# A decoder layer on eight cores: the weight tiles become one stream, and each load is queued when its slot is released

## The chip, the cores and the metric

The kernel runs on the 8 cores of one Trainium2 chip. Every core runs the same program on its own tokens, and no core waits for another. The metric is the device time of the slowest core in microseconds (us); the median of three runs before the change is 3491.16 us (3490.33 to 3492.99).

## The reference

One layer of a hybrid decoder, and a final norm:

```
x += 0.5 * SwiGLU(rms(x)) @ w_down                     # FFN1, width 5632
h  = rms(x);  p = h @ w_in                             # u, v, glu_a, glu_b, gate_a, gate_b
u  = gelu(ua);  v = layer_norm(gelu(va))
y_a = (u * (causal W_s per head and 128-chunk @ v + b_s)) @ w_pa
g  = glu_a * sigmoid(glu_b)                            # 2048 channels
c  = silu(layer_norm(depthwise_conv(g, 31 taps)))      # causal; sample rows take their past from cache_conv
y_b = c @ w_pb
x += (sig(gate_a) * y_a + sig(gate_b) * y_b) @ w_out
x += 0.5 * SwiGLU(rms(x)) @ w_down                     # FFN2
y  = rms(x)
```

The model width is 2048. There are 4 prompts of 2048 tokens and 128 running sequences of 4 new tokens. The outputs are y, the last rows of v and the last 30 rows of the convolution's input.

## The kernel before

Each core holds 1118 tokens (1024 of a prompt, 64 of samples, 30 that the convolution needs from the half prompt before) as columns of [channel, token] tiles, in three segments s = 0, 1, 2 of 364, 364 and 390 columns. All tiles lie in one SBUF tensor, `arena`, and all PSUM banks in `ps`, so these are the names that the profile prints. `mm`, `act`, `tt` and `stt` are helpers that record one operation each; so nearly every matmul has line 192, and every DMA of the program has line 949.

**Weights.** They stream from DRAM (f32) into four SBUF slots (bf16, 128x4096) with DMAs issued by GpSimd (POOL). `wload` (lines 217 to 220) takes the next slot of the ring and queues, on POOL, the wait for the matmul that released that slot and then the DMA. It is called where the tile's use is written; POOL's queue runs in the order in which it was written.

**Stages.** FFN1 (gate-up and down tiles), then the GLU with the convolution, then v (`w_v`), u (`w_u`) with the spatial product, then the gates and both branch projections (`w_gate`, `w_pab`), `w_out`, FFN2. POOL issues weight loads in all of them, and besides them only the small tables `mskc` and `wp` in FFN1 and the convolution's cache rows, below.

**GLU and convolution** (lines 456 to 585), for 16 channel tiles c. GLU(c) is 96 matmuls with the weight tile `w_glu[c]`: for each segment the gate half, then the linear half, multiplied on VectorE into `GP[c % 3]`. `glu_out(c)` writes that tile to DRAM (`gd`) and the state rows to `cst`; `glu_in()` reads it back in four DMAs, shuffled over the partitions, into `GPB[c % 3]`. conv(c) is 72 matmuls over `GPB` and `GS`; its result goes to DRAM (`cd`) and comes back in four DMAs. All of these are issued by SyncE (SP), whose queue is also in written order with its waits: write of `gd`, wait, 4 reads, then write of `cd` once conv is evicted, wait, 4 reads. `conv_weights(c)` (VectorE, two operations of 128x2304) builds the convolution's stationary operand. `conv_cache(c)` is a POOL DMA of the cache rows, `arena<-cachep`, into `GS[c % 3]`; it waits until the convolution that used this buffer, three tiles earlier, is done (`gs_free`).

The order of the stage is written out by hand: GLU(0) to GLU(2) run segment by segment on three tiles held at once, then `conv_cache` for 0, 1 and 2; then for c = 3 to 15 this loop, in which c = 4 and c = 5 run two convolutions each and every other c runs one:

```
for c in range(SKEW, KC):                    # 570
    wi, slot, lev = wload(w_glu[c], 4096)
    ...                                      # GLU(c)
    for cc in order.get(c, [c - 1]):
        conv(cc)
        ...
            cg[cc + 3] = conv_cache(cc + 3)  # 584
```

Of the kernel before, what the change touches and what calls it, by code (L numbers as in the profile page):

```python
# [11 lines left out]
KC = 16  # L12
# [13 lines left out]
SKEW = 3  # L26
# [72 lines left out]
def build_program():  # L99
# [42 lines left out]
    P = Plan()  # L142

    with nc.sbuf_tensor("arena", [128, ARENA_B // 4], F32) as arena, \
# [69 lines left out]
        def pvc(g, k):  # L214
            return PV[:, g * 16 + k:g * 16 + k + 1]

        def wload(src, n, after=()):
            idx, slot, free = wring.get()
            ev = P.dma("pool", slot[:, 0:n], src, "w%d" % idx, deps=free + list(after))
            return idx, slot, ev  # L220

        def wk(slot):
            return slot[:, 0:4096].rearrange("p (k n) -> p k n", n=256)
# [58 lines left out]
                steps.pop(0)()  # L282


        def ffn(w_gu, w_dn, segs, Hv, HID, Xs, hready, seg_steps, tail_steps, dn_seg, x_final, hook, first_order):
            hid = {}
            hid_free = {0: None, 1: None, 2: None}

            def unit(slot, lev, jj, s, steps):
                x0, n = segs[s]  # L290
                W = wk(slot)
                gi_, bg, gfree = banks.get()
                ui_, bu, ufree = banks.get()
                lg = lu = None
                for k in range(KC):
                    lg = mm(bg[:, 0:n], W[:, k, 0:128], Hv[:, k, x0:x0 + n], k == 0, k == KC - 1,
                            deps=[lev, hready[(s, k)]] + (gfree if k == 0 else []))
# [12 lines left out]
                return lu  # L310

            def down(W, m, mi, s, lev):
                x0, n = segs[s]
                bi, bk, bfree = banks.get()
                ld = None
                for jj in range(11):
                    ld = mm(bk[:, 0:n], W[:, jj, mi * 128:(mi + 1) * 128], HID[:, jj, x0:x0 + n], jj == 0, jj == 10,
                            deps=[lev, hid[s]] + (bfree if jj == 0 else []))
                ed = stt(Xs[s][:, m, 0:n], bk[:, 0:n], 0.5, Xs[s][:, m, 0:n], ALU.mult, ALU.add, deps=[ld])
                banks.release(bi, [ed])  # L320
                hid_free[s] = ld
                return ld, ed

            for gi in range(4):
                if gi == 0:
                    held = []
                    for jj in range(SKEW):
                        held.append(wload(w_gu[jj], 4096, after=hook("w", jj)))
                        hook("wl", jj, held[jj][2])
                    for (s, jj) in first_order:  # L330
                        wi, slot, lev = held[jj]
                        if (s, jj) == (1, 0):
                            run_steps(seg_steps.get(1, []), 99)
                        if (s, jj) == (2, 0):
                            run_steps(seg_steps.get(2, []), 99)
                        nxt = 1 if (s, jj) in first_order[:first_order.index((1, 0))] else 2
                        lu = unit(slot, lev, jj, s, seg_steps.get(nxt, []) if s < 2 else [])
                        if s == 2:
                            wring.release(wi, [lu])
                for jj in range(SKEW if gi == 0 else 0, 11):  # L340
                    wi, slot, lev = wload(w_gu[gi * 11 + jj], 4096)
                    lu = None
                    for s in range(3):
                        lu = unit(slot, lev, jj, s, [])
                    wring.release(wi, [lu])
                nm = 8 if gi < 3 else 8 - dn_seg
                for mp in range(nm):
                    wi, slot, lev = wload(w_dn[gi * 8 + mp], 2816)
                    W = slot[:, 0:2816].rearrange("p (j n) -> p j n", n=256)
                    ld = None  # L350
                    for mi in range(2):
                        for s in range(3):
                            ld, ed = down(W, mp * 2 + mi, mi, s, lev)
                            if gi == 3:
                                x_final[(s, mp * 2 + mi)] = ed
                    wring.release(wi, [ld])
                hook("g", gi)
                if gi == 3:
                    held = []
                    for mp in range(nm, 8):  # L360
                        held.append((mp,) + wload(w_dn[gi * 8 + mp], 2816))
                    for s in range(3):
                        for (mp, wi, slot, lev) in held:
                            W = slot[:, 0:2816].rearrange("p (j n) -> p j n", n=256)
                            for mi in range(2):
                                ld, ed = down(W, mp * 2 + mi, mi, s, lev)
                                x_final[(s, mp * 2 + mi)] = ed
                                if s > 0:
                                    run_steps(tail_steps[s - 1], 3)
                            if s == 2:  # L370
                                wring.release(wi, [ld])
                        if s > 0:
                            run_steps(tail_steps[s - 1], 99)
                        hook("s", s)
# [11 lines left out]
        def hook1(what, i, ev=None):  # L386
# [37 lines left out]
            return []  # L424

        run_steps(steps1[0], 99)
        ffn(w_gu1, w_dn1, SEG_A, H, HID1, X1, h1, {1: steps1[1], 2: steps1[2]}, stepsm, DN_SEG, x1f, hook1,
            [(0, 0), (0, 1), (1, 0), (1, 1), (0, 2), (1, 2), (2, 0), (2, 1), (2, 2)])


# [118 lines left out]
                          cd[c].rearrange("(i c) g n -> g c i n", i=4)[g], "cr%d" % (c % 4), deps=[wv])  # L549
            cn_ev[c] = r  # L550

        held = [wload(w_glu[c], 4096) for c in range(SKEW)]
        for s in range(3):
            for c in range(SKEW):
                wi, slot, lev = held[c]
                la = glu_unit(c, slot, lev, s, stepsm[2])
                if s == 2:
                    wring.release(wi, [la])
                    if c == 0:
                        x1_dead = [hm[(0, 15)], hm[(1, 15)], hm[(2, 15)]] + list(sp_ev.values())  # L560
                    glu_out(c)
                    glu_in()
# [5 lines left out]
        cw[1] = conv_weights(1)  # L568
        order = {3: [0], 4: [1, 2], 5: [3, 4]}
        for c in range(SKEW, KC):  # L570
            wi, slot, lev = wload(w_glu[c], 4096)
            la = None
            for s in range(3):
                la = glu_unit(c, slot, lev, s, [])
            wring.release(wi, [la])
            glu_out(c)
            glu_in()
            for cc in order.get(c, [c - 1]):
# [117 lines left out]
                                deps=[e, e_mv])  # L696

        for nb in range(8):
            wi, slot, lev = wload(w_v[nb], 4096)
            W = wk(slot)  # L700
            lm = None
            for (t, rows, hc) in vt:
# [10 lines left out]
                if nb >= 1:  # L713
                    if side:
                        run_steps(side, 3)
                    else:
                        run_steps(side_b, 1)
            wring.release(wi, [lm])
        run_steps(side, 99)
        run_steps(side_b, 99)  # L720

# [75 lines left out]
            u_free[c % 2] = [us_ev[c]]  # L797

        for cp_ in range(8):
            wi, slot, lev = wload(w_u[cp_], 4096)  # L800
            W = wk(slot)
            lm = None
            for ci in range(2):
# [7 lines left out]
                if c == 2:  # L811
                    od8 = v_out(VT[1], 64, vsamp_o, e_vt8, "o_vs")
                    us_after = [od7, od8]
            wring.release(wi, [lm])
        spatial(KC - 1)


# [4 lines left out]
        m_ev = None  # L822
        lya = None
        for c in range(KC):
            w2i, slot2, lev2 = wload(w_gate[c], 4096)
            w1i, slot1, lev1 = wload(w_pab[c], 4096)
            W1 = wk(slot1)
            W2 = wk(slot2)
            for s in range(3):
# [27 lines left out]
                banks.release(yai, [e1])  # L857
                SAR.release(sai, [e1])
                m_ev = tt(MM_[:, c, x0:x0 + n], ta[:, 0:n], tb[:, 0:n], ALU.add, deps=[e1, e2])
            wring.release(w2i, [lgb])  # L860
            wring.release(w1i, [lya])


        rl = {}
# [19 lines left out]

        OUT_SEG = 3
        for mp in range(8 - OUT_SEG):
            wi, slot, lev = wload(w_out[mp], 4096)
# [4 lines left out]
            wring.release(wi, [lm])  # L892
        held = [(mp,) + wload(w_out[mp], 4096) for mp in range(8 - OUT_SEG, 8)]
        for s in range(3):
            for (mp, wi, slot, lev) in held:
                for mi in range(2):
# [1 line left out]
                    if s > 0:  # L898
                        run_steps(steps2[s - 1], 3)
                if s == 2:  # L900
                    wring.release(wi, [lm])
            if s > 0:
                run_steps(steps2[s - 1], 99)

# [5 lines left out]
        def hook2(what, i, ev=None):  # L910
            return []

        ffn(w_gu2, w_dn2, SEG_B, H2, HID2, X2, h2, {1: steps2[2]}, stepsf, 3, x3f, hook2,
            [(s, jj) for s in range(3) for jj in range(SKEW)])
        run_steps(stepsf[2], 99)
        for s in range(3):
# [180 lines left out]
```

How the kernel before makes its waits and increments, by code:

```python
            def emit(eng, e):  # L935
                for item in P.q[eng]:
                    if item[0] == "wait":
                        k, v = item[1], item[2]
                        if k in esem:
                            e.wait_ge(esem[k], sigval[k][v])
                        else:
                            e.wait_ge(dsem[k], v)
                    elif item[0] == "op":
                        ins = item[1](e)
                        idx = item[2]
                        if eng in sigval and idx in sigval[eng]:
                            ins.then_inc(esem[eng], 1)
                    else:
                        ins = e.dma_start(out=item[1], in_=item[2])
                        ins.then_inc(dsem[item[3]], 16)
```

## Time and profile before

| | |
|---|---|
| median of the runs (range) | 3491.16 us (3490.33 to 3492.99) |
| the profiled execution: its own time, span of its slowest core | 3496.27 us, 3494.7 us |
| spans of the eight cores | 3480.9 to 3494.7 us |
| TensorE (PE) busy | 3253.0 us, 93% |
| VectorE (DVE), ScalarE (ACT), GpSimd (POOL) busy | 856.9, 466.4, 128.1 us |
| mean granted TensorE clock | 0.966 |

The span is from the first to the last instruction on core 2, the slowest in this execution. PE is busy nearly all the time, so the time of the kernel is that of PE's work plus the idle time in front of it. "A <- B" in a row is: A was idle and B was what it waited for last. A granted clock of 1.00 is 2.4 GHz, one of 0.50 is 1.2 GHz.

### The profile page before, as it was taken

The numbers are of one execution on the slowest core, as the hardware profiler recorded it, in microseconds if no ns is written. First come the engines' busy times: TensorE is split into PE (matmuls) and PEld (weight loads), VectorE is DVE, ScalarE is ACT, GpSimd is POOL, SyncE is SP. The second block draws the span as 40 slices with busy tenths as digits, with TensorE's granted clock in tenths as the row PEclk, the third lists the DMA queues.
The fourth block names the chain that finished last, engine by engine and source line by source line (L and its number), as shares of the span: only waits on it lengthen the run. The fifth ranks groups of instructions, "written<-read, shape, count | busy, mean of one in ns | idle before, by whom it ended". The sixth has DMA issues, their size and how long they took to land.

```text
span 3494.7 us, 51300 instructions; the slowest of 8 cores (3480.9 to 3494.7 us)
## 1 busy us (share of the span) xinstructions
PE 3253.0 (93%) x21555; PEld 2067.1 (59%) x21556; DVE 856.9 (25%) x1448; ACT 466.4 (13%) x909; POOL 128.1 (4%) x246
## 2 busy tenths in 40 slices
PE   6999999999999756579899999999999999999997
PEld 2566666666665434347756666666666666666664
DVE  2212122121126221222643111112412112112115
ACT  3000000000003100014721000000300000000002
POOL 0000000000000000000000000000000000000000
PEclk9999999999999878789999999999999999999998
DMA  6436434334345343352344334337333434434434
GB/s 155 74 61 123 80 59 81 69 66 85 66 103 127 67 85 55 78 115 59 65 87 73 71 70 71 71 69 177 58 72 71 84 63 78 73 58 82 73 63 119
DMA packets 74112, 284.30 MB, mean 81 GB/s; under 512 B 9888, under 2 KB 36768, under 8 KB 52000
## 3 DMA queue, kind: packets, MB, share of 16 engines
q0 software_dynamic: 34848, 216.62, 35.6%
q1 hardware_dynamic: 39040, 64.40, 6.3%
q8 instruction: 176, 2.88, 0.3%
q14 instruction: 48, 0.39, 0.0%
HBM read 468.14 MB, written 32.87 MB: 143 GB/s over the span
## 4 chain that ended last, share of the span: by engine, by line
PE 91%; DMA 5%; DVE 2%; ACT 1%; issue 1%; POOL 0%; SPq 0%; DVEq 0%; ACTq 0%; POOLq 0%
PE ps L192 91%; DMA arena<-w_glu 4%; ACT arena L195 1%; DVE arena L205 1%; DMA arena<-xin 1%; ACT L195 0%; DVE arena L209 0%; DVE arena L198 0%; DMA vsamp<-arena 0%; DMA arena<-gd 0%; POOL arena L949 0%; DMA gd<-arena 0%; SPq L949 0%; DVEq L940 0%; DVE arena L201 0%
## 5 line engine op out<-in xcount | busy, mean ns | idle before, releaser
L192 PE MATMUL ps<-arena 128*128 128x364 bf16 (+5 forms) x21555 | 3253.0, 313 | 220.7 <-DMA arena<-w_glu 141.6
L192 PEld LDWEIGHTS ps<-arena 128*128 128x128 bf16 (+1 forms) x21556 | 2067.1, 98 | 1406.5 <-issue 282.4
L198 DVE TENSOR_TENSOR arena<-arena,ps 128x364 bf16<-128x364 f32 (+9 forms) x472 | 237.0, 515 | 1838.9 <-PE ps L192 1836.4
L195 ACT ACTIVATE arena<-ps 128x364 f32<-128x364 f32 (+1 forms) x528 | 241.5, 463 | 2574.4 <-PE ps L192 2524.5
L205 DVE SCALAR_TENSOR_TENSOR arena<-ps,arena 128x364 f32<-128x364 f32 (+5 forms) x451 | 241.1, 539 | 501.2 <-PE ps L192 500.9
L198 DVE TENSOR_TENSOR arena<-arena 128x512 bf16<-128x512 f32 (+7 forms) x168 | 185.3, 1115 | 67.3 <-PE ps L192 44.2
L195 ACT ACTIVATE arena<-arena 128x364 bf16<-128x364 f32 (+6 forms) x276 | 152.8, 631 | 268.5 <-PE ps L192 191.7
L205 DVE SCALAR_TENSOR_TENSOR arena<-arena 128x364 bf16<-128x364 f32 (+4 forms) x196 | 101.2, 594 | 1.8 <-DVE arena L209 0.2
L949 POOL DMA_DIRECT2D arena<-w_gu x88 | 46.6, 529 | 1173.3 <-PE ps L192 1132.8
L949 POOL DMA_DIRECT2D arena<-w_dn x64 | 33.8, 528 | 773.8 <-PE ps L192 761.6
L195 ACT ACTIVATE arena<-ps,arena 128x272 bf16<-128x272 f32 (+3 forms) x76 | 38.0, 500 | 102.9 <-PE ps L192 102.8
L209 DVE RECIPROCAL arena<-arena 128x364 f32<-128x364 f32 (+4 forms) x14 | 36.6, 2612 | 42.6 <-ACT arena L195 42.6
L198 DVE TENSOR_TENSOR arena<-ps,arena 128x364 f32<-128x364 f32 (+1 forms) x48 | 24.9, 534 | 87.2 <-PE ps L192 70.0
L195 ACT ACT_TABLE_LOAD x29 | 37.2, 1283 | 62.1 <-PE ps L192 48.2
L691 DVE BATCH_NORM_STATS2 arena<-arena 128x6 f32<-128x256 bf16 (+1 forms) x72 | 26.9, 411 | 59.8 <-ACT arena L195 59.8
L949 POOL DMA_DIRECT2D arena<-cachep x16 | 8.5, 530 | 426.6 <-PE ps L192 386.6
L949 POOL DMA_DIRECT2D arena<-w_gate x16 | 8.4, 528 | 369.2 <-PE ps L192 369.2
L949 POOL DMA_DIRECT2D arena<-w_pab x16 | 8.4, 528 | 91.3 <-PE ps L192 91.3
L949 POOL DMA_DIRECT2D arena<-w_glu x16 | 8.6, 536 | 41.8 <-PE ps L192 41.6
L949 POOL DMA_DIRECT2D arena<-w_u x8 | 4.2, 528 | 153.3 <-PE ps L192 153.3
L949 POOL DMA_DIRECT2D arena<-w_v x8 | 4.3, 538 | 147.2 <-PE ps L192 147.2
L201 DVE TENSOR_SCALAR arena<-ps 128x364 f32<-128x364 f32 (+1 forms) x3 | 1.6, 536 | 31.2 <-PE ps L192 31.2
(10 smaller groups left out, 15.9 us busy)
## 6 DMA issues: line engine op xcount, KB each, us to landing
arena<-w_gu POOLq DMA_DIRECT2D x88, 1024.0 KB, 8.1
arena<-w_dn POOLq DMA_DIRECT2D x64, 704.0 KB, 6.2
arena<-w_glu POOLq DMA_DIRECT2D x16, 1024.0 KB, 11.7
arena<-w_gate POOLq DMA_DIRECT2D x16, 1024.0 KB, 8.7
arena<-w_pab POOLq DMA_DIRECT2D x16, 1024.0 KB, 9.8
arena<-w_v POOLq DMA_DIRECT2D x8, 1024.0 KB, 9.6
arena<-w_u POOLq DMA_DIRECT2D x8, 1024.0 KB, 8.1
arena<-w_out POOLq DMA_DIRECT2D x8, 1024.0 KB, 10.3
```

The lines of the kernel that those rows point to most:

```text
L192: return P.op("pe", lambda e: e.matmul(out, lhsT, rhs, start=start, stop=stop), deps)
L195: return P.op("act", lambda e: e.activation(out=out, in_=in_, func=func, **kw), deps)
L198: return P.op("dve", lambda e: e.tensor_tensor(out=out, in0=in0, in1=in1, op=op), deps)
L201: return P.op("dve", lambda e: e.tensor_scalar(out=out, in0=in0, scalar1=s1, scalar2=s2, op0=op0, op1=op1), deps)
L205: return P.op("dve", lambda e: e.scalar_tensor_tensor(out=out, in0=in0, scalar=scalar, in1=in1, op0=op0, op1=op1), deps)
L209: return P.op("dve", lambda e: e.reciprocal(out=out, in_=in_), deps)
L691: e = P.op("dve", lambda e, t=t, rows=rows, nb=nb: e.bn_stats(out=VST[0:rows, t, nb * 6:nb * 6 + 6], in_=V[0:rows, t, nb * 256:(nb + 1) * ...
L949: ins = e.dma_start(out=item[1], in_=item[2])
```

## The change

The order of all 252 weight tiles is written down once (`wseq`). `wissue` queues the next tile's load; `wnext` hands out the oldest tile that was issued; `wdone` releases a slot and calls `wissue` right there. The first four loads are queued at the start of FFN1, and from then on each load is queued where the slot that it takes is released: four tiles ahead of its use. No operation is added or removed on any engine, and the number and size of the slots stay. What moves is where the loads stand in POOL's queue, relative to `mskc`, `wp` and `cachep`.

```diff
-        def wload(src, n, after=()):
-            idx, slot, free = wring.get()
-            ev = P.dma("pool", slot[:, 0:n], src, "w%d" % idx, deps=free + list(after))
-            return idx, slot, ev
+        wseq = []
+        for gu, dn in ((w_gu1, w_dn1), (None, None), (w_gu2, w_dn2)):
+            if gu is None:
+                wseq += [(w_glu[c], 4096) for c in range(KC)]
...
+        wahead = []
+
+        def wissue(after=()):
+            if wseq:
+                src, n = wseq.pop(0)
+                idx, slot, free = wring.get()
+                wahead.append((idx, slot, P.dma("pool", slot[:, 0:n], src, "w%d" % idx, deps=free + list(after))))
+
+        def wnext():
+            return wahead.pop(0)
+
+        def wdone(idx, events):
+            wring.release(idx, events)
+            wissue()
...
-                        held.append(wload(w_gu[jj], 4096, after=hook("w", jj)))
+                        if not wahead:
+                            wissue(hook("w", jj))
+                        held.append(wnext())
                         hook("wl", jj, held[jj][2])
+                    if not wahead:
+                        wissue()
...
-        held = [wload(w_glu[c], 4096) for c in range(SKEW)]
+        held = [wnext() for c in range(SKEW)]
         for s in range(3):
             for c in range(SKEW):
                 wi, slot, lev = held[c]
                 la = glu_unit(c, slot, lev, s, stepsm[2])
                 if s == 2:
-                    wring.release(wi, [la])
+                    wdone(wi, [la])
...
         for c in range(SKEW, KC):
-            wi, slot, lev = wload(w_glu[c], 4096)
+            wi, slot, lev = wnext()
             la = None
             for s in range(3):
                 la = glu_unit(c, slot, lev, s, [])
-            wring.release(wi, [la])
+            wdone(wi, [la])
```

The other uses of `wload` and `wring.release` become `wnext` and `wdone` in the same way.

POOL's queue of before, from the end of FFN1's loads to the loop's c = 8; `s_pe` is a wait for TensorE, `s_dve` for VectorE, `d_xs..` for the DMAs that save x1 to DRAM:

```order
L949 DMA arena<-w_glu 128x4096 [waits s_pe] x3
L949 DMA arena<-cachep 128x512 [waits s_dve,d_xsa0,d_xsa1,d_xsa2,d_xsb0,d_xsb1,d_xsb2]
L949 DMA arena<-cachep 128x512 x2
L949 DMA arena<-w_glu 128x4096 [waits s_pe]
L949 DMA arena<-cachep 128x512 [waits s_pe]
L949 DMA arena<-w_glu 128x4096
L949 DMA arena<-cachep 128x512 [waits s_pe] x2
L949 DMA arena<-w_glu 128x4096
L949 DMA arena<-cachep 128x512 [waits s_pe] x2
L949 DMA arena<-w_glu 128x4096
L949 DMA arena<-cachep 128x512 [waits s_pe]
L949 DMA arena<-w_glu 128x4096
```

The same place in POOL's queue of the changed kernel:

```order
L976 DMA arena<-w_glu 128x4096 [waits s_pe] x7
L976 DMA arena<-cachep 128x512 [waits s_dve,d_xsa0,d_xsa1,d_xsa2,d_xsb0,d_xsb1,d_xsb2]
L976 DMA arena<-cachep 128x512 x2
L976 DMA arena<-w_glu 128x4096 [waits s_pe]
L976 DMA arena<-cachep 128x512 [waits s_pe]
L976 DMA arena<-w_glu 128x4096 [waits s_pe]
L976 DMA arena<-cachep 128x512 [waits s_pe] x2
L976 DMA arena<-w_glu 128x4096 [waits s_pe]
L976 DMA arena<-cachep 128x512 [waits s_pe] x2
L976 DMA arena<-w_glu 128x4096 [waits s_pe]
```

Seven `w_glu` loads instead of three now stand ahead of the first cache rows. A load that follows a cache row has a wait for TensorE of its own (its slot's release, GLU(c)); before, it had none left, because the cache row just ahead of it had already waited for something later, the end of a convolution. The loads `w_glu[4]` to `w_glu[14]` each stood behind the cache row whose convolution ended just before the load was needed; now the load that follows that row is for a tile four further on.

The end of the loop, in POOL's queue of before:

```order
L949 DMA arena<-w_glu 128x4096
L949 DMA arena<-cachep 128x512 [waits s_pe]
L949 DMA arena<-w_glu 128x4096
L949 DMA arena<-cachep 128x512 [waits s_pe]
L949 DMA arena<-w_glu 128x4096 x2
L949 DMA arena<-w_v 128x4096 x2
L949 DMA arena<-w_v 128x4096 [waits s_pe] x6
```

And of the changed kernel:

```order
L976 DMA arena<-w_glu 128x4096 [waits s_pe]
L976 DMA arena<-cachep 128x512 [waits s_pe]
L976 DMA arena<-w_v 128x4096 [waits s_pe]
L976 DMA arena<-cachep 128x512 [waits s_pe]
L976 DMA arena<-w_v 128x4096 [waits s_pe]
L976 DMA arena<-cachep 128x512 [waits s_pe]
L976 DMA arena<-w_v 128x4096 [waits s_pe] x6
```

`w_v[0]` and `w_v[1]` move ahead of the last two cache rows; `w_v[2]` and all later loads stand behind the same work as before. The queues of TensorE, VectorE, ScalarE and SyncE have the same instructions in the same order in both kernels.

## Rows read from the trace of the kernel before

**Rows 1.** All cores: span and mean granted clock.

```profile
core 2: 3494.7 us, clock 0.966
core 3: 3490.3 us, clock 0.966
```

**Rows 2.** Waits of PE, whole span: total us, times, longest us.

```profile
PE ps L192 <- DMA arena<-w_glu: 141.6, 11, 13.5
PE ps L192 <- ACT arena L195: 46.2, 19, 7.8
...
PE ps L192 <- DMA arena<-gd: 8.6, 1, 8.6
```

**Rows 3.** Chain of waits, 1290 to 1350 us: start us, us, what.

```profile
1299.00 11.86 DMA arena<-w_glu
...
1311.10 21.66 PE ps L192 x168
```

**Rows 4.** Timeline of POOL, 1294 to 1312 us: start us, us, operation, idle before.

```profile
1298.48 0.53 POOL L949 DMA_DIRECT2D arena<-cachep  x1 [33.83 <-PE ps L192]
1299.00 0.54 POOL L949 DMA_DIRECT2D arena<-w_glu  x1
```

**Rows 5.** Windows after one stall: busy us per engine, then clock, DMA share, GB/s.

```profile
1311.00:1314.00 3.00, 2.90 (x10) 1.48 (x11) 0.00 (x0) 0.00 (x0) 0.00 (x0) 0.50 0.00 1
...
1318.00:1323.00 5.00, 5.00 (x34) 3.12 (x33) 0.93 (x2) 0.47 (x1) 0.00 (x0) 1.00 0.02 3
```

**Rows 6.** Windows: from GLU(3)'s end to GLU(14)'s, and on to GLU(15)'s.

```profile
1142.50:1540.40 397.90, 256.28 (x1994) 168.87 (x1993) 95.62 (x103) 41.16 (x85) 14.78 (x28) 0.80 0.41 77
1540.40:1560.40 20.00, 20.00 (x170) 13.65 (x169) 7.79 (x9) 3.39 (x7) 0.00 (x0) 1.00 0.53 113
```

**Rows 7.** Timeline of SP's queue on core 2, 1538 to 1563 us.

```profile
1540.42 0.34 SPq L949 DMA_DIRECT2D gd<-arena  x1
...
1550.46 1.74 SPq L949 DMA_DIRECT2D arena<-gd  x4
1552.30 0.38 SPq L949 DMA_DIRECT2D cd<-arena  x1
1554.61 1.73 SPq L949 DMA_DIRECT2D arena<-cd  x4
1560.43 0.34 SPq L949 DMA_DIRECT2D gd<-arena  x1
```

**Rows 8.** The same queue on core 2, 1130 to 1150 us: GLU(3)'s write.

```profile
1142.50 0.34 SPq L949 DMA_DIRECT2D gd<-arena  x1
```

**Rows 9.** The same queue on core 3: the writes of GLU(3) and of GLU(14).

```profile
1144.13 0.34 SPq L949 DMA_DIRECT2D gd<-arena  x1
...
1536.11 0.34 SPq L949 DMA_DIRECT2D gd<-arena  x1
```

**Rows 10.** Timeline of PE, 1505 to 1605 us: conv(12) alone.

```profile
1504.80 4.89 PE L192 MATMUL ps<-arena 128*128 128x256 bf16 x71
```

**Rows 11.** Timeline of POOL, 1538 to 1582 us: the load issued at GLU(14)'s end.

```profile
1539.62 0.53 POOL L949 DMA_DIRECT2D arena<-w_v  x1 [26.75 <-PE ps L192]
```

**Rows 12.** Tile w_v, 1512 to 1513 us: third and fourth of four loads in a row.

```profile
DMA to landing us min/median/max: 24.6/26.9/29.2
```

**Rows 13.** DMAs, 1540 to 1560 us: median us from issue to landing last.

```profile
arena<-w_v POOLq DMA_DIRECT2D x1, 1024.0 KB, 10.4
gd<-arena SPq DMA_DIRECT2D x1, 280.0 KB, 9.9
arena<-gd SPq DMA_DIRECT2D x4, 70.0 KB, 2.0
```

**Rows 14.** Tile cd, 1302 to 1306 us: four reads beside a weight load.

```profile
DMA to landing us min/median/max: 7.0/7.3/7.4
```

**Rows 15.** Chain of waits, 1500 to 1580 us: the last step of GLU(15)'s round trip.

```profile
1565.66 6.68 DMA arena<-gd
```

**Rows 16.** Windows: FFN1, PE without a gap.

```profile
97.00:1058.00 961.00, 960.89 (x6078) 587.49 (x6078) 173.66 (x315) 67.84 (x142) 39.58 (x75) 1.00 0.44 82
```

More of the change, by code:

```diff
@@ L215, in pvc @@
             return PV[:, g * 16 + k:g * 16 + k + 1]
-        def wload(src, n, after=()):
-            idx, slot, free = wring.get()
-            ev = P.dma("pool", slot[:, 0:n], src, "w%d" % idx, deps=free + list(after))
-            return idx, slot, ev
+        wseq = []
+        for gu, dn in ((w_gu1, w_dn1), (None, None), (w_gu2, w_dn2)):
+            if gu is None:
+                wseq += [(w_glu[c], 4096) for c in range(KC)]
+                wseq += [(w_v[c], 4096) for c in range(8)] + [(w_u[c], 4096) for c in range(8)]
+                for c in range(KC):
+                    wseq += [(w_gate[c], 4096), (w_pab[c], 4096)]
+                wseq += [(w_out[c], 4096) for c in range(8)]
+            else:
+                for gi in range(4):
+                    wseq += [(gu[gi * 11 + jj], 4096) for jj in range(11)]
+                    wseq += [(dn[gi * 8 + mp], 2816) for mp in range(8)]
+        wahead = []
[9 more added lines that the diff above has]
+            wissue()
         def wk(slot):
@@ L282, in run_steps, with ffn @@
                 steps.pop(0)()
-        def ffn(w_gu, w_dn, segs, Hv, HID, Xs, hready, seg_steps, tail_steps, dn_seg, x_final, hook, first_order):
+        def ffn(segs, Hv, HID, Xs, hready, seg_steps, tail_steps, dn_seg, x_final, hook, first_order):
             hid = {}
@@ L338, in ffn @@
                         if s == 2:
-                            wring.release(wi, [lu])
+                            wdone(wi, [lu])
                 for jj in range(SKEW if gi == 0 else 0, 11):
-                    wi, slot, lev = wload(w_gu[gi * 11 + jj], 4096)
+                    wi, slot, lev = wnext()
                     lu = None
@@ L344, in ffn @@
                         lu = unit(slot, lev, jj, s, [])
-                    wring.release(wi, [lu])
+                    wdone(wi, [lu])
                 nm = 8 if gi < 3 else 8 - dn_seg
                 for mp in range(nm):
-                    wi, slot, lev = wload(w_dn[gi * 8 + mp], 2816)
+                    wi, slot, lev = wnext()
                     W = slot[:, 0:2816].rearrange("p (j n) -> p j n", n=256)
@@ L355, in ffn @@
                                 x_final[(s, mp * 2 + mi)] = ed
-                    wring.release(wi, [ld])
+                    wdone(wi, [ld])
                 hook("g", gi)
@@ L360, in ffn @@
                     for mp in range(nm, 8):
-                        held.append((mp,) + wload(w_dn[gi * 8 + mp], 2816))
+                        held.append((mp,) + wnext())
                     for s in range(3):
@@ L370, in ffn @@
                             if s == 2:
-                                wring.release(wi, [ld])
+                                wdone(wi, [ld])
                         if s > 0:
@@ L426, in build_program @@
         run_steps(steps1[0], 99)
[L427 removed]
+        ffn(SEG_A, H, HID1, X1, h1, {1: steps1[1], 2: steps1[2]}, stepsm, DN_SEG, x1f, hook1,
             [(0, 0), (0, 1), (1, 0), (1, 1), (0, 2), (1, 2), (2, 0), (2, 1), (2, 2)])
@@ L570, in build_program @@
         for c in range(SKEW, KC):
-            wi, slot, lev = wload(w_glu[c], 4096)
+            wi, slot, lev = wnext()
             la = None
@@ L698, in build_program @@
         for nb in range(8):
-            wi, slot, lev = wload(w_v[nb], 4096)
+            wi, slot, lev = wnext()
             W = wk(slot)
@@ L717, in build_program @@
                         run_steps(side_b, 1)
-            wring.release(wi, [lm])
+            wdone(wi, [lm])
         run_steps(side, 99)
@@ L799, in build_program @@
         for cp_ in range(8):
-            wi, slot, lev = wload(w_u[cp_], 4096)
+            wi, slot, lev = wnext()
             W = wk(slot)
@@ L813, in build_program @@
                     us_after = [od7, od8]
-            wring.release(wi, [lm])
+            wdone(wi, [lm])
         spatial(KC - 1)
@@ L824, in build_program @@
         for c in range(KC):
-            w2i, slot2, lev2 = wload(w_gate[c], 4096)
-            w1i, slot1, lev1 = wload(w_pab[c], 4096)
+            w2i, slot2, lev2 = wnext()
+            w1i, slot1, lev1 = wnext()
             W1 = wk(slot1)
@@ L859, in build_program @@
                 m_ev = tt(MM_[:, c, x0:x0 + n], ta[:, 0:n], tb[:, 0:n], ALU.add, deps=[e1, e2])
-            wring.release(w2i, [lgb])
-            wring.release(w1i, [lya])
+            wdone(w2i, [lgb])
+            wdone(w1i, [lya])
         rl = {}
@@ L886, in build_program @@
         for mp in range(8 - OUT_SEG):
-            wi, slot, lev = wload(w_out[mp], 4096)
+            wi, slot, lev = wnext()
             lm = None
@@ L891, in build_program @@
                     lm = out_unit(wk(slot), mi, mp * 2 + mi, s, lev)
-            wring.release(wi, [lm])
-        held = [(mp,) + wload(w_out[mp], 4096) for mp in range(8 - OUT_SEG, 8)]
+            wdone(wi, [lm])
+        held = [(mp,) + wnext() for mp in range(8 - OUT_SEG, 8)]
         for s in range(3):
@@ L900, in build_program @@
                 if s == 2:
-                    wring.release(wi, [lm])
+                    wdone(wi, [lm])
             if s > 0:
@@ L911, in hook2 @@
             return []
-        ffn(w_gu2, w_dn2, SEG_B, H2, HID2, X2, h2, {1: steps2[2]}, stepsf, 3, x3f, hook2,
+        ffn(SEG_B, H2, HID2, X2, h2, {1: steps2[2]}, stepsf, 3, x3f, hook2,
             [(s, jj) for s in range(3) for jj in range(SKEW)])
```

## The prediction

> **What bounds the kernel now.** I read the waits of PE first, because PE is busy for 93% of the span. Its largest wait is for `w_glu` loads: 141.6 us in 11 waits, so 12.9 us each [rows 2]. The next, 46.2 us for ScalarE, lies in the v stage, which the change leaves in its order; the rest is small. So the GLU and convolution stage is where the change can act.
>
> The chain of waits shows one such stall: a `w_glu` load takes 11.86 us to land, and only then do PE's next 168 matmuls start, GLU(c) and the convolution behind it [rows 3]. The timeline of POOL shows why the load came late. POOL sat idle for 33.83 us until PE was done with the last convolution, issued the cache rows it had been waiting for, and 0.52 us later the weight load [rows 4]. The slot had been free all that time: the load itself has no wait left in the queue (POOL's order in the section on the change). So the wait for `gs_free`, which belongs to the cache rows, holds up a load that PE needs at once. This happens before GLU(4) to GLU(14), 11 times, as counted.
>
> The windows show a second cost. When PE restarts, the granted clock is 0.50 (1.2 GHz) for the first 3 us, in which 10 matmuls run; further on it is 1.00 [rows 5]. PE had been idle for 13 us before.
>
> **What the new stretch takes.** The best row is in this trace. From GLU(14) on there is no cache row left in the queue and the weights are ahead. Between the `gd` writes of GLU(14) and GLU(15) lie 1560.43 - 1540.42 = 20.01 us [rows 7], in which PE runs conv(13) and GLU(15) (168 matmuls) with no gap at clock 1.00 [rows 6]. And this turn has just the load pattern that the change gives to all others: one weight load (`w_v[2]`) issued at GLU's end. A convolution alone takes 4.89 us at full clock [rows 10], so a GLU takes 15.1.
>
> On core 2, from GLU(3)'s write to GLU(14)'s it is 1540.42 - 1142.50 = 397.9 us [rows 7, 8]. After: 11 turns of one convolution and one GLU, and two turns (behind c = 4 and 5) have a second convolution: 11 x 20.01 + 2 x 4.89 = 229.9 us. That is 168.0 us less: 141.6 of waits [rows 2], and by difference 26.4 us of slow clock, 2.4 us per restart (10 matmuls in 2.9 us at half clock, and as long or somewhat longer again, cost that much).
>
> **From one core to the time.** The slowest core of before isn't that of after, since the stalls differ by core. On core 3 the same stretch takes 1536.11 - 1144.13 = 392.0 us [rows 9], so it gains 162.1; its span of 3490.3 becomes 3328.2, core 2's 3494.7 becomes 3326.7 [rows 1]. The others, worked out in the same way, come to 3323 to 3328, and core 3 is the slowest. The profiled execution is 1.57 us longer than its span, so it would be 3329.8, that is 166.5 us below its own 3496.27. That execution lies 5.1 us above the median of 3491.16, and I take the difference from the median: 3491.16 - 166.5 = 3324.7. If the 5.1 us lie outside the stretch I still keep them off; if the offset comes back whole, the time is 3329.8, an upper bound.
>
> **What is moved, and what covers it.**
>
> - *Weight loads, one per turn, now at GLU's end.* They have four turns (80 us) to land against 10 to 12 us. Hidden entirely. If that cover went, 12.9 us each come back.
> - *Cache rows*: issued where they were, at the end of a convolution, but now behind a weight load issued 5 us before. They land a little later than that load, 12 us after GLU's end, and are used two turns later. Behind a waiting cache row only loads stand that have three turns of slack. Hidden.
> - *The first cache rows* are the exception, since they now stand behind `w_glu[4]` to `[6]`. Counting back from GLU(3)'s end at 1141.7 (a GLU's end is 0.8 before its write, as 1539.6 before 1540.42 [rows 7, 11]) by 15.1 us, GLU(0) to GLU(2) release their slots at about 1116, 1121 and 1127 (the third segment is 390 of 1118 columns, 5.3 us of a GLU). Of four loads in a row the third landed 24.6 us after its own issue, so 25.7 after the first's, at 0.53 per issue [rows 11, 12]: so the third load here lands by 1142 at worst, and the rows a few us after. conv(0) wants them at about 1143, after its first 9 matmuls. Between 0 and 3 us, once; the loads are spaced here and not issued at once, so I take 1.
> - *SP's transfers meet the weight load.* Before, the load was issued at conv's end, when the `gd` round trip was over. Now it is issued 0.8 us ahead of the write of `gd`. The trace has this case: with `w_v[2]` in flight, landing after 10.4 us, the 280 KB write took 9.9 [rows 13]. A small transfer behind a weight load lands when the load does; the reads of `cd` tell the same, 7.0 to 7.4 us beside a load against 2.0 for those of `gd` without one [rows 13, 14]. From GLU's end at 1539.6 [rows 11]: write landed at 1550.3, four reads issued until 1552.2 and landed 2.0 us later, 1554.2; conv(14) starts at 1559.6. So 5.4 us to spare. SP's own turn ends with the reads of `cd` at 1556.3, 4.1 us before the next write [rows 7]. Both fit, so 0 in the sum. The bound from above: reads that take 7.4 us even so would land at 1559.2 to 1559.6, still just in time.
> - *VectorE and ScalarE*: busy 7.79 and 3.39 of 20 us in that turn [rows 6]. No bound.
> - *conv(15)'s wait of 8.6 us* [rows 2] is GLU(15)'s round trip [rows 15], with `w_v[3]` issued at the same point in both. It stays; it moves by 2 us either way with the order in which the write and the load reach the engines.
> - *All other stages*: POOL's queue holds nothing but weight loads there, so queuing earlier does not issue them earlier; `mskc` and `wp` wait for long finished work. 0.
>
> The Trainium skill, "DMA: Bandwidth & Descriptors", section "Queues, rings and completion order", says that each DMA engine takes turns between the queues that have work, packet by packet. By that the `gd` write would take perhaps twice what it does alone, and the spare time would be some 5 us more. This trace disagrees, 9.9 us beside a load of 10.4 [rows 13]; by either the sum is the same, and by the page the first rival would be next to impossible. I go by the rows.
>
> Sum: 3324.7 + 1 = 3326 us.
>
> **The rivals.**
>
> 1. *The DRAM round trip becomes the bound of a turn* (chance 0.11). With the stalls gone, 20 us must hold what had 35: write, reads, write, reads, in SP's written order, all beside a load. For it: 16.7 of 20 us of SP's queue are used, and the turns of all eight cores come closer together, so landings may lengthen. Against it: the turn measured above, and a DMA share of only 0.53 in it [rows 6]. It decides from 4 to 5 us of lengthening; each us beyond costs 9 turns (the two with a second convolution have 4.9 us more). 3 us beyond: 27 us, 3353.
> 2. *The wait goes, but the slow clock stays* for part of the stretch (0.03), if short waits of PE remain. It gives back up to 26.4 us: 3352. Against: FFN1 runs 961 us at 1.00 [rows 16].
> 3. *It does not do what it says* (0.02): loads still land just before use, since waiting cache rows still stand ahead of them. Against: POOL's order, in which each load behind a cache row is for a tile three turns later. 3491.
> 4. *Slower* (0.02): the denser stretch is granted clock 0.50 throughout. A turn is then twice 20.01 us, 40.0 against 35.3 before (11 turns in 397.9 less 9.8); that is +52 us, 3543. It decides when over three quarters of the stretch runs at half clock. Against: the clock of 1.00 in [rows 6, 16].
>
> My forecast has the remaining 0.82: every load hidden, the clock full, one or no wait at the start, 3320 to 3334.
>
> **How the numbers follow.** 3326 is the likeliest. Its own range adds the bounds: 2 us for the first cache rows, 2 for conv(15), and the 5.1 of the profiled execution above; below, 5 us for cores that end earlier. I stretch the range to 3342 for the start of rival 1 (up to 2 us a turn). Faster by more than 0.2% (7 us, about what a measurement of this kernel tells from no change): 0.82 + 0.11 + 0.03 = 0.96. Within 0.2%: 0.02. Slower: 0.02.
>
> **What would show it.** In the changed kernel's profile PE's waits have no `w_glu`; `gd` writes of consecutive tiles are 20 us apart, and from GLU(3) to GLU(14) it is 230 us; the granted clock of that stretch is 1.00; writes of `gd` take about 10 us to land; one wait for `gd` of 7 to 11 us stays before conv(15), and at most one of 3 us for `cachep` before conv(0). I am wrong if PE waits for `gd` in each turn, if SP's writes follow one another with no idle time, or if the clock stays below 0.95.

## The result: 4.3% faster, and the profile after

The ratio of the time after to the time before is 0.9567, with a 95% interval of 0.9548 to 0.9586. All times here and below are of executions in which no die ran markedly longer at a lower clock than the other: four of the changed kernel, 3339.07 to 3341.33 us, and three of before, 3490.33 to 3492.99. That is 3340.5 against 3491.2 us, 151 us less; forecast were 3326 and 165. The profiled execution took 3340.61 us; its slowest core is core 4, with a span of 3339.1 us.

PE's waits in the changed kernel, over the span of core 4 (total us, times, longest):

```profile
PE ps L192 <- ACT arena L195: 48.5, 19, 10.1
PE ps L192 <- DVE arena L205: 16.8, 13, 5.3
PE ps L192 <- DMA arena<-gd: 12.6, 2, 9.1
PE ps L192 <- DVE arena L198: 3.6, 2, 2.2
```

The 141.6 us for `w_glu` [rows 2] are gone. ScalarE's part is the same within 2.3 us. New are a second wait for `gd` (3.5 us) and one for VectorE (2.2 us, in the row of line 198); the wait of 9.1 us for `gd` is conv(15)'s, as before.

The queue of SyncE in one turn, GLU(6)'s write to GLU(7)'s, on core 4:

```profile
1223.37 0.34 SPq L976 DMA_DIRECT2D gd<-arena  x1
...
1233.28 1.74 SPq L976 DMA_DIRECT2D arena<-gd  x4
1235.12 0.38 SPq L976 DMA_DIRECT2D cd<-arena  x1
1237.47 1.73 SPq L976 DMA_DIRECT2D arena<-cd  x4
1243.39 0.34 SPq L976 DMA_DIRECT2D gd<-arena  x1
```

This is the turn of [rows 7] again, 20.02 us, with the write of `gd` under way for nearly 10 us and 4.2 us of SP's queue free at the end. The seven turns behind it, as a window (PE, PEld, DVE, ACT, POOL busy; clock; DMA share; GB/s):

```profile
1243.40:1383.50 140.10, 140.10 (x1178) 95.66 (x1177) 54.53 (x63) 23.77 (x49) 7.42 (x14) 1.00 0.58 119
```

PE has no gap, the granted clock is 1.00 (2.4 GHz) where it was 0.80 [rows 6], and seven turns take 140.1 us, 20.01 each. The chain of waits of the stage, core 4 (start us, us, what):

```profile
1142.95 0.40 DVE arena L198
...
1145.42 2.24 DVE arena L198
...
1147.89 3.27 DVE arena L198 x2
...
1151.29 250.94 PE ps L192 x2142
...
1403.56 3.98 DMA gd<-arena
...
1409.03 6.90 DMA arena<-gd
```

From 1151.29 on PE alone makes the chain for 251 us, to the end of GLU(15); the round trip at the end is the one of [rows 15]. The loss lies ahead of it, at conv(0).

**The start of the loop.** The timeline of POOL on core 4:

```profile
1118.12 0.53 POOL L976 DMA_DIRECT2D arena<-w_glu  x1 [41.82 <-PE ps L192]
1123.39 0.53 POOL L976 DMA_DIRECT2D arena<-w_glu  x1 [4.75 <-PE ps L192]
1128.67 0.53 POOL L976 DMA_DIRECT2D arena<-w_glu  x1 [4.75 <-PE ps L192]
1129.65 1.59 POOL L976 DMA_DIRECT2D arena<-cachep  x3 [0.45 <-issue]
...
1157.66 0.53 POOL L976 DMA_DIRECT2D arena<-cachep  x1 [13.00 <-PE ps L192]
```

In the chain of waits a DMA issue on POOL follows its release by some 0.5 us. So GLU(2) was over at 1128.2, and with 15.1 us for GLU(3) and 4.9 for conv(0) the latter should have ended at 1148.2; it ended at 1157.2, 9.0 us late. The DMAs issued from 1117 to 1160 us, median us to landing last:

```profile
arena<-w_glu POOLq DMA_DIRECT2D x4, 1024.0 KB, 11.9
gd<-arena SPq DMA_DIRECT2D x4, 280.0 KB, 9.9
arena<-gd SPq DMA_DIRECT2D x12, 70.0 KB, 7.6
...
cst<-arena SPq DMA_DIRECT2D x3, 47.0 KB, 12.0
```

Two kinds of these are waited for. The reads of `gd` for tile 0, issued once its write had landed after 13.4 us, from the view of that tile:

```profile
  PE ps L192: 3.5, 1
...
DMA to landing us min/median/max: 10.8/11.5/12.3
```

And VectorE, from its waits between 1100 and 1160 us:

```profile
DVE arena L198 <- DMA cst<-arena: 10.3, 1, 10.3
```

GLU(2)'s state rows use the buffer of GLU(0)'s (`GTF[c % 2]`), whose write to `cst`, issued at 1119.28 us, takes 20.2 us:

```profile
L976 SPq DMA_DIRECT2D cst<-arena x1: 425/425/425, 1119.3 to 1119.3; - x1
...
DMA to landing us min/median/max: 20.2/20.2/20.2
```

VectorE's queue stands for 10.3 us. Behind it wait the convolution weights for c = 0 and 1 (9.97 us) and then GLU(3)'s products, whose PSUM banks conv(0) needs: PE waits 2.2 us for them. The waits sum to 5.7 us. Most of the rest of the 9.0 goes with a slower clock; windows from GLU(3) to the end of conv(0), columns as above:

```profile
1128.20:1143.40 15.20, 15.09 (x96) 9.01 (x94) 4.17 (x7) 1.45 (x3) 2.12 (x4) 1.00 1.01 163
1143.40:1147.40 4.00, 0.61 (x4) 0.45 (x5) 4.00 (x2) 0.00 (x0) 0.53 (x1) 0.79 1.18 211
1147.40:1151.30 3.90, 1.70 (x17) 1.23 (x16) 3.90 (x4) 0.49 (x1) 0.00 (x0) 0.50 0.85 113
1151.30:1153.30 2.00, 2.00 (x13) 1.40 (x14) 1.60 (x6) 0.00 (x0) 0.00 (x0) 0.50 0.91 181
1153.30:1155.30 2.00, 2.00 (x19) 1.45 (x18) 0.00 (x0) 0.49 (x1) 0.00 (x0) 0.50 0.95 238
1155.30:1157.30 2.00, 2.00 (x32) 1.66 (x30) 0.07 (x1) 0.57 (x2) 0.00 (x0) 0.83 0.46 143
```

After the first wait PE runs at a granted clock of 0.50 (1.2 GHz) until 1155.3. The DMA share is 1.01 in the first window: while the loads for tiles 4 to 6 are in flight, the DMA engines have no idle time left, against 0.58 in the ordinary turns.

The eight cores do not lose the same. On cores 1, 3, 4 and 6 the `cst` write of tile 0 takes 18.9 to 20.2 us, PE has both waits, and conv(0) ends 8.1 to 9.2 us late; on the other four it takes 8.2 to 8.6 us, only the wait for `gd` is there, and conv(0) ends 4.4 to 6.1 us late.

### The profile page after: what moved, and what is told of

The parts are those of the page before. It is cut to its first block, busy times and chain, and to the rows that moved or that the text cites. A ratio compares the mean times of both kernels' runs of the same rounds, so it can differ in the third digit from the quotient of the medians.

```text
span 3339.1 us, 51314 instructions; the slowest of 8 cores (3331.6 to 3339.1 us)
## 1 busy us (share of the span) xinstructions
PE 3232.5 (97%) x21555; PEld 2059.6 (62%) x21556; DVE 856.8 (26%) x1448; ACT 467.0 (14%) x909; POOL 128.6 (4%) x246
## 4 chain that ended last, share of the span: by engine, by line
PE 94%; DVE 2%; ACT 1%; DMA 1%; issue 1%; SPq 0%; DVEq 0%; ACTq 0%
PE ps L192 94%; ACT arena L195 1%; DVE arena L205 1%; DMA arena<-xin 1%; DVE arena L198 1%; ACT L195 0%; DVE arena L209 0%; DMA vsamp<-arena 0%; DMA arena<-gd 0%; DMA gd<-arena 0%; SPq L976 0%; DVEq L967 0%; DVE arena L201 0%; DVEq L953 0%; ACTq L967 0%
## 5 line engine op out<-in xcount | busy, mean ns | idle before, releaser
(10 smaller groups left out, 15.9 us busy)
## 6 DMA issues: line engine op xcount, KB each, us to landing
arena<-w_glu POOLq DMA_DIRECT2D x16, 1024.0 KB, 10.3
```

## The experiments

**1. The cache rows' place alone.** The kernel of before; each cache row is queued after the next weight load:

```diff
             wi, slot, lev = wload(w_glu[c], 4096)
+            while late:
+                cl = late.pop(0)
+                cg[cl] = conv_cache(cl)
...
-                    cg[cc + 3] = conv_cache(cc + 3)
+                    late.append(cc + 3)
```

> The kernel of before with one edit: in the loop the cache rows of a convolution are queued on POOL after the next weight load instead of ahead of it. No stream, loads one tile ahead. Theory (the wait for the cache rows' buffer was all that held the loads; nothing else of the stream matters): no wait for w_glu before GLU(4) to GLU(14), and since only w_glu[4] stands in front at the start of the loop, the start of the stage is not crowded: 3330 to 3336 us, up to 9 us below the changed kernel's 3340.5. Rival (four tiles ahead are needed): waits for w_glu of 3 us or more per tile remain, 3370 us or more.

Measured: 3338.46 to 3339.25 us, ratio 0.9557 (0.9538 to 0.9576), no wait for `w_glu` left. So this one reordering gives the whole gain, and no stream is needed. The start was clean, as expected (0.6 us of waits at most on any core from 1090 to 1200 us), but the time is not the 3330 to 3336 that I expected, because of the other end. POOL and SP on its slowest core, core 2:

```profile
1359.17 0.54 POOL L953 DMA_DIRECT2D arena<-w_glu  x1
1359.69 1.07 POOL L953 DMA_DIRECT2D arena<-w_v  x2
```

```profile
1374.62 0.34 SPq L953 DMA_DIRECT2D gd<-arena  x1
...
1391.44 1.74 SPq L953 DMA_DIRECT2D arena<-gd  x4
```

Here three loads go out at once at the end of the loop, and `w_v[2]` follows at 1373.83 us. Three are in flight when GLU(14)'s write of `gd` is issued at 1374.62 (the load of `w_glu[15]` has landed, at 1371.0), and that write takes 16.7 us to let the reads go. PE waits 11.6 us for `gd` before conv(15) on this core and 2.0 us before conv(14), instead of 8.6 once. The crowd only stands elsewhere.

**2. Order or distance.** The changed kernel; in the loop a load is queued behind the turn's cache rows again, still four tiles ahead:

```diff
-            wdone(wi, [la])
+            wring.release(wi, [la])
...
                 if cc + 3 < KC:
                     cg[cc + 3] = conv_cache(cc + 3)
+            wissue()
```

> The changed kernel with the loop's weight loads queued behind the convolutions and their cache rows again, but still four tiles ahead. Theory (a load that stands behind the cache rows costs nothing when its tile is needed three turns later; what mattered is the distance, not the order): no wait for w_glu, the write of gd lands in 2 to 4 us instead of 10, and the time is that of the changed kernel within 3 us, 3337 to 3342, since the crowded start is unchanged. Rival (the order of load and cache rows itself brings the gain): waits for w_glu return, 3400 us or more.

Measured: 3338.39 to 3341.66 us, the changed kernel's time. Its DMAs from 1220 to 1380 us:

```profile
gd<-arena SPq DMA_DIRECT2D x8, 280.0 KB, 2.1
...
cd<-arena SPq DMA_DIRECT2D x8, 272.0 KB, 6.4
```

The write of `gd`, no longer beside a load, lands in 2.1 us; that of `cd`, now beside it, takes 6.4. Neither is waited for in an ordinary turn. So a load may stand behind a waiting cache row as long as its tile is needed turns later: being "ahead of the cache rows" is one way to get the distance and not what counts.

**3. The slow clock by itself.** The kernel of before, with PE kept busy in the stalls:

```diff
+            if c < 14:
+                for _ in range(72):
+                    mm(ps[:, 7, 0:364], ONES, H[:, 0, 0:364], True, True,
+                       deps=stat_banks.free[0] + stat_banks.free[1])
```

> The kernel of before with 72 matmuls of 364 columns, whose result nobody reads, queued on PE behind the convolutions of c = 3 to 13; they fill some 11 of the 12.9 us in which PE waits for the next w_glu load. The loads come as late as before. Theory (the stage also loses about 26 us because PE restarts at half clock after each stall): the granted clock stays near 1.00 in the loop and the time falls by 15 to 26 us although no load comes earlier: 3466 to 3477. Rival (the slow clock is not caused by the stalls, or costs nothing; the whole gain of the change is the waits): 3491 or more.

Measured: 3473.25 and 3473.90 us, 18 below before. PE does 792 matmuls more, and the loads still wait for each convolution. Its wait for the loads, and the window over the stage on the slowest core:

```profile
PE ps L192 <- DMA arena<-w_glu: 17.5, 11, 3.0
```

```profile
1146.00:1530.00 384.00, 366.53 (x2846) 242.74 (x2844) 101.45 (x106) 42.34 (x88) 14.78 (x28) 0.99 0.41 83
```

The clock is 0.99 instead of 0.80. So the second cost of a stall, the restart at 1.2 GHz, is real: of the 26.4 us that I put on it, 18 show up here. Where the other 8 went, this run does not show.

**4. Three state-row buffers.** The changed kernel with `GTF[c % 3]`:

```diff
-        GTF = [view(OFF_T + 19040 + i * 376, [94]) for i in range(2)]
+        GTF = [view(OFF_T + 19040, [94]), view(OFF_T + 19416, [94]), view(OFF_T + 24448, [94])]
```

> The changed kernel with three buffers instead of two for the state rows (GTF), so that GLU(2) does not wait for the cst write of GLU(0). Theory (two things are late behind the three weight loads at the start of the loop: the gd round trip of tile 0, and the cst write that VectorE waits for, which delays the building of the convolution's weights): VectorE's wait of 10.3 us goes and PE's wait for VectorE in conv(0) with it, 2 to 6 us below the changed kernel: 3334 to 3338. Rival (only the gd read decides): same as the changed kernel, 3340.

Measured: 3338.39 to 3339.91 us, at most 2 below the changed kernel and within its scatter. That misses the 3334 to 3338 that I expected; by the time, the rival holds. No core has a wait of PE for VectorE at conv(0) any more (cores 1, 3, 4 and 6 had one), while the wait for `gd` (2.2 to 3.9 us) stays on all eight. So the `cst` write was the cause of that one wait, but it is not shown that removing it alone gains anything.

**5. The first loads spread.** None is issued by GLU(0) to GLU(2); one call stands behind the first cache rows, two more behind the convolutions of c = 4 and 5:

```diff
                 if s == 2:
-                    wdone(wi, [la])
+                    wring.release(wi, [la])
...
+        wissue()
         cw[0] = conv_weights(0)
...
+            if c in (4, 5):
+                wissue()
```

> The changed kernel with the loads of w_glu[4] to [6] spread: none is issued when GLU(0) to GLU(2) release their slots; one is issued behind the first cache rows, the others during c = 4 and 5. From c = 5 on the queue is four ahead as in the changed kernel. Theory (the 9 us that PE loses at conv(0) on core 4 come from those three loads standing in front of the small transfers): no wait for gd or VectorE at conv(0), 3330 to 3335 us, 6 to 10 below the changed kernel. Rival (the loss is the ordinary turn's, a gd write beside one load): unchanged, 3340.

Measured: 3334.27 to 3335.27 us, 6 below the changed kernel: the loss, or this much of it, is the crowd's. It was a partial cure. `w_glu[5]`, queued by GLU(3), takes the slot that GLU(1) released, so POOL still issues two loads 5.3 us apart, and four cores kept a wait for VectorE of 3.0 to 3.4 us and no wait for `gd`.

**6. Spread more.** As above, but one load behind each convolution's cache rows up to c = 5, and three state-row buffers:

```diff
                 if cc + 3 < KC:
                     cg[cc + 3] = conv_cache(cc + 3)
+                if c <= 5:
+                    wissue()
```

> The changed kernel with the first loads of the loop spread further: one (w_glu[4]) behind the first cache rows, then one behind each convolution's cache rows up to c = 5, and from c = 6 on as in the changed kernel; and three state-row buffers. Theory (crowding at the loop's start is all that the changed kernel lost against the forecast): no wait of PE at conv(0) on any core, 3328 to 3332 us. Rival (what is left is spread over other stages): 3335 to 3340 as with the loads spread less.

Measured: 3337.53 to 3339.50 us, against the expectation. Nothing waits at conv(0), but the turns of c = 4 and 5 now carry two loads each. SP on core 6, where GLU(5)'s reads end the round trip:

```profile
1176.41 0.93 SPq L981 DMA_DIRECT2D cd<-arena  x1
1190.79 1.73 SPq L981 DMA_DIRECT2D arena<-cd  x4
1192.62 0.38 SPq L981 DMA_DIRECT2D gd<-arena  x1
...
1196.54 2.72 SPq L981 DMA_DIRECT2D arena<-gd  x4
```

The write of `cd` took 14.3 us and held up everything behind it in SP's queue; the reads for conv(5) then landed late and PE waited 4.3 us. This is the first rival's mechanism, brought about by a second load in a turn.

**7. The last round trip.** Experiment 6, and `w_v[3]` waits for the reads of conv(15):

```diff
-            if c > 5:
+            if 5 < c < KC - 1:
                 wissue()
             glu_out(c)
             glu_in()
+            if c == KC - 1:
+                wissue([sh[c]])
```

> The kernel of the run e6_spread_and_buffers with one more edit: the load issued at the end of GLU(15), w_v[3], waits until the reads of gd for conv(15) have landed. Theory (a small transfer beside a weight load lands when the load does, and that is most of PE's wait of 7 to 9 us for gd before conv(15)): that wait falls to 2 to 4 us, 4 to 6 us below e6. Rival (the wait is the round trip's own latency): no change.

Measured: 3330.95 to 3332.37 us, 7 below experiment 6, where I expected 4 to 6. PE's wait before conv(15) is 3.2 to 4.7 us on the eight cores instead of 6.7 to 9.5: about half of it was the load and not the trip. What gives the other 2 to 3 us is not shown. The wait behind the doubly loaded turns stays, 1.7 to 3.3 us.

**8. Each load twice.** The changed kernel with `w_glu[9]` to `[14]` loaded a second time once the first load has landed:

```diff
+                ev = P.dma("pool", slot[:, 0:n], src, "w%d" % idx, deps=free + list(after))
+                if len(wseq) in twice:
+                    ev = P.dma("pool", slot[:, 0:n], src, "w%d" % idx, deps=[ev])
```

> The changed kernel with the loads of w_glu[9] to [14] each issued a second time into the same slot, once the first has landed, so that in the turns from GLU(5) to GLU(10) a weight load is in flight nearly all of the 20 us. Theory (the round trip through DRAM had 5 us to spare in an ordinary turn, and a small transfer beside a load lands with the load): the turn grows to 22 to 25 us with waits for gd or late writes, 3350 to 3370 us. Rival (the DMA engines share evenly between the queues, so a load in flight costs small transfers little): turns stay at 20.0 us, 3340.

Measured: 3353.51 and 3356.82 us, 13 to 16 above the changed kernel. PE's waits on the slowest core:

```profile
PE ps L192 <- DMA arena<-gd: 30.5, 5, 12.4
```

The waits at conv(0) and conv(15) are among the five. So an ordinary turn has no room for a second load, and a load in flight does cost the small transfers. On that core the five writes of `gd` from 1232.6 to 1318.9 us are 21.6 us apart on average, so a turn grew by 1.6, less than the 2 to 5 I expected. The turns did not grow evenly: one wait there is of 12.4 us, as is one of 11.6 on core 6, and on the other six cores the waits of all the doubled turns sum to 4.4 to 7.6. The run also raises the DMA share of these turns, to 0.77, so it does not tell the order of the transfers from the mere amount.

**9 and 10. All causes together.** Experiment 9 is experiment 5 with three state-row buffers and `w_v[3]` held. Experiment 10 holds each of the first three loads until the reads of `gd` of its tile's convolution have landed, queued behind the first cache rows, with the same two other edits:

```diff
                 if s == 2:
-                    wdone(wi, [la])
+                    wring.release(wi, [la])
...
+        for c in range(3):
+            wissue([sh[c]])
         cw[0] = conv_weights(0)
```

> The changed kernel with the first loads spread as in e5_spread_first_loads, three state-row buffers, and w_v[3] held until the reads of gd for conv(15) have landed. Theory (three causes that add up: crowding at the start, the two state buffers, the load beside the last round trip): no wait before conv(15)'s, that one 3 to 4 us; 3326 to 3330 us. Rival (one of the three takes over what another gives back): 3331 to 3335 as in the runs of e5 and e7.

> The changed kernel with w_glu[4], [5] and [6] held until the reads of gd for conv(0), conv(1) and conv(2) have landed, queued behind the first cache rows; three state-row buffers; w_v[3] held as in e7_last_load_held. From GLU(3) on the loop is the changed kernel's, so each turn has its weight load beside the write of gd. Theory (loads hurt only where small transfers of several tiles queue behind several loads): no wait for gd at conv(0), 3326 to 3331 us. Rival (the backlog of the start is only moved to conv(1) to conv(3)): a wait for gd there of 3 us or more, 3332 to 3338.

Measured: 3329.24, 3329.95, 3330.24 and once 3338.35 us for experiment 9; 3327.90, 3328.78, 3330.27 and once 3340.15 for experiment 10. The one higher time of each lies in an execution in which two cores have a mean clock of 0.981 against 0.989 and take 12 to 16 us longer; neither was profiled, their cause is open, and I leave them aside. The others are 10 to 13 us below the changed kernel. The two versions can't be told apart: the ratios to before, with the higher times in, are 0.9528 (0.9508 to 0.9548) and 0.9531 (0.9506 to 0.9556). Experiment 9's expectation holds (3326 to 3330 us, at its upper end), experiment 10's too. PE's waits for DMA on the slowest core of experiment 10 come down to one:

```profile
PE ps L192 <- DMA arena<-gd: 4.6, 1, 4.6
```

No core of experiment 10 has any wait of PE from 1090 to 1340 us. The backlog is not moved to conv(1) to conv(3) as the rival had it.

## Why the prediction was right, and where it was off

The measured 3340.5 us lies outside the 3320 to 3334 that the chance of 0.82 stood for. It is in the range only by the stretch to 3342, which was put in for turns lengthened by up to 2 us each. The turns did not lengthen; the time came there through the start of the loop. That the range covers it is luck.

- *The cause of the stalls* was right. Moving the cache rows alone removes them (experiment 1). One reading beside it was wrong: ScalarE's 46.2 us do not all lie in the v stage; 24.4 of them lie before 1100 us, in FFN1, and 17.4 between 1580 and 2000. They barely moved, so the sum does not change.
- *What the turn takes* was right to 0.1%: 20.01 us forecast, 20.02 and 20.01 measured. The row that gave it was a turn which already ran under the conditions of the change [rows 7].
- *The clock*: the granted clock is 1.00, and the stalls were its cause (experiment 3). The turn's length already held this gain, so its share of 26.4 us did not enter the sum by itself.
- *SP's transfers beside a load*: 9.6 us measured at the median for `gd` in the ordinary turns of the changed kernel, against 9.9 in the row, and nothing waits. The first rival did not come about in these turns. It does in turns with more than one load in flight (experiments 6 and 8). The rival's 16.7 us of SP's queue were counted from GLU's end; from its own first write to its last read they are 15.9 [rows 7].
- *The first cache rows* is the term that was mis-sized: I took 1 us, from 0 to 3, and it measured 9.0 on core 4 and 5.8 on core 0. The load's row was read rightly, but I looked only for what the cache rows would meet. The `gd` and `cst` transfers of tiles 0 to 2 share the DMA engines with the same three loads, and the `cst` write holds a buffer that VectorE needs. I had costed "beside one load" for SP and never for three. This is the first rival's mechanism at one place, once, with some 3 us of the second's (the slow clock behind the wait), and worth 8 us more than the sum had. Spreading the loads gives 6 of them back (experiment 5), and holding them removes the waits (experiment 10, whose other gain is conv(15)'s).
- *From the profiled execution to the median*: I kept its offset of 5.1 us off. The changed kernel's profiled execution has no such offset (3340.61 in 3339.07 to 3341.33). Seventeen executions of before over the study lie between 3490.2 and 3497.1, the four of the changed kernel within 2.3 us. That fits an offset that lay in the stalls, which the change removes; then it should not have been subtracted. This is argued, not shown: in the session of experiments 9 and 10 four more of before took 3499.4 to 3503.3, and there kernels without stalls show a higher time as well, so at least that offset is not the stalls'. By the execution's own time, 3329.8 and 9.0 us for the start, the sum is 3338.8, against 3340.61. Core by core the two sides fit unevenly. Core 3, forecast 3328.2 and with its 8.9 us at the start 3337.1, measured 3336.2. Core 4, forecast in the same way 3325.8 and with 9.0 us 3334.8, measured 3339.1. It reached the end of GLU(2) 1.1 us later and waited 0.5 us longer before conv(15); the last 2.7 us are not traced.
- *conv(15)'s wait* stayed, 9.1 us against 8.6.
- *The rivals 2, 3 and 4* (clock stays slow, no effect, slower) are ruled out for the stage by the window and the waits.
- *The signs*: no wait for `cachep` came at conv(0) but one for `gd`, and on four cores one for VectorE. The 230 us from GLU(3) to GLU(14) can't be read from the `gd` writes, since GLU(3)'s stood in SP's late queue; from GLU(3)'s end to GLU(14)'s it is 238.6 us, 8.7 more, nearly all at conv(0).

## What to carry to other kernels

A load behind a wait that belongs to something else is late by that wait. It is enough that nothing with a late wait stands between a slot's release and a load needed soon; a load for a later tile may stand behind it. Where loads are made early, look at the place where the pipeline fills: there several are in flight together, and every small transfer that someone waits for, even an output's, lands late, here after 13.4 and 20.2 us. Cost each such transfer there, not only in the ordinary turn.

## What the runs showed of the hardware

A transfer issued just after a 1 MB weight load, by another queue, lands about when the load does: the 280 KB write of `gd` in 9.9 us beside a load of 10.4 [rows 13], in 2.1 us without one (experiment 2), and in 16.7 with three in flight (experiment 1). Issued ahead of the load it depends on by how much. GLU(15)'s write in the changed kernel, 0.8 us ahead, took 3.98 us, after which the reads took 6.9. In experiment 2 the writes of `cd` that were issued 0.3 to 0.4 us ahead of the load took 3.8 to 5.3 us and one 0.1 us ahead took 9.9, against 2.3 without a load.

This bears out what I took from the rows against the turn-taking in the Trainium skill, "DMA: Bandwidth & Descriptors", section "Queues, rings and completion order": one write beside one load takes far more than twice its time alone. The same section of the Trainium skill also says that a semaphore's increment lands only after every earlier write of that DMA engine, across its queues. The trace agrees with that, 9.9 us for a later transfer and 3.98 for one ahead of the load.

A plain queue in the order of issue does not fit all of it. On core 4 of the changed kernel the `cst` write of tile 0, issued at 1119.28 us, landed at 1139.5, and the load issued at 1123.39, 4.1 us behind it, had landed at 1136.0; cores 1, 3 and 6 show the same. What orders the landings in such a crowd is open.

PE's restart after a stall of some 13 us runs at 1.2 GHz for its first 3 us or more [rows 5]; in the changed kernel it does so at conv(0) from 1147.4 to 1155.3 us, after a wait of 3.5 us and with one of 2.2 us in between. Filling the pauses with useless matmuls, 792 in all, made the kernel 18 us faster.
